# Gated delta rule on one core: where the steps of the neighbouring projections stand among the waits of the chunk inverse

## What is computed

```
proj = h @ w_in                      # q, k (8 heads), v, z (16 heads), b, a
q, k, v = silu(causal_conv(...));  q, k are normalised
a_low = strict((k*beta) @ k.T * decay)        # chunks of 64 tokens
t_inv = inverse(eye + a_low)
u = t_inv @ (v*beta);  w = t_inv @ (k*beta*exp(gc))
per chunk: v_new = u - w @ state
           o = q_dec @ state + attn_intra @ v_new
           state = state*exp(gl) + k_tail.T @ v_new
x = x + (rmsnorm(o) * silu(z)) @ w_o
```

## Time and profile before

| | us |
|---|---|
| median of 3 runs | 1586.14 (1583.64 to 1587.31) |
| the profiled execution, its own time | 1573.19 |
| its span | 1571.4 |
| PE busy | 1516.2 (96% of the span) |
| DVE busy | 560.7 (36%) |
| ACT busy | 378.9 (24%) |
| POOL busy | 189.1 (12%) |
| mean granted TensorE clock | 0.989 of full speed |

### The profile page before, as it was taken

How to read it: one execution, slowest core, us unless ns; L and a number is a source line. 1 busy time by engine, 2 the same in 40 slices (tenths; PEclk the granted TensorE clock), 3 DMA queues, 4 the chain that set the end, 5 groups by cost and what they waited for, 6 DMA issues and landing times.

```text
span 1571.4 us, 34876 instructions
## 1 busy us (share of the span) xinstructions
PE 1516.2 (96%) x15613; PEld 897.7 (57%) x15613; DVE 560.7 (36%) x802; ACT 378.9 (24%) x603; POOL 189.1 (12%) x182
## 2 busy tenths in 40 slices
PE   8799999998999998999999999999999999999997
PEld 6677888776878786753533534444434335345344
DVE  4645444576766757332211212121111112111113
ACT  5544444473645454220000000000000000000000
POOL 0100000114342516000000000000000000000100
PEclk9899999999999999999999999999999999999999
DMA  9218555543142300499999999999999999999993
GB/s 350 92 53 273 188 187 188 163 158 108 55 135 81 132 4 1 156 415 408 411 410 408 411 411 409 410 410 397 411 413 403 412 402 409 412 389 413 414 404 159
DMA packets 145354, 450.38 MB, mean 287 GB/s; under 512 B 10624, under 2 KB 41888, under 8 KB 130880
## 3 DMA queue, kind: packets, MB, share of 16 engines
q1 hardware_dynamic: 141680, 437.10, 72.0%
q0 software_dynamic: 3536, 11.14, 1.8%
HBM read 440.87 MB, written 7.34 MB: 285 GB/s over the span
## 4 chain that ended last, share of the span: by engine, by line
PE 86%; DVE 8%; issue 2%; ACT 1%; SPq 1%; DMA 1%; POOL 1%; POOLq 0%; DVEq 0%; ACTq 0%
PE banks L1929 37%; PE banks L1946 19%; PE banks L1452 8%; PE banks L1454 7%; PE banks L1453 7%; PE banks L1849 1%; PE banks L1839 1%; DVE cvall L1139 1%; DVE wlo L955 1%; PE banks L1830 1%; DMA par<-in_attn_sinks_dram 1%; DVE T L1199 1%; SPq L409 1%; PE banks L1886 1%; PE banks L1858 0%
## 5 line engine op out<-in xcount | busy, mean ns | idle before, releaser
L1929 PE MATMUL banks<-ring,xg 128*32 128x512 f32 (+1 forms) x6144 | 583.2, 539 | 0.0
L1929 PEld LDWEIGHTS banks<-ring,xg 128*32 128x32 f32 x6144 | 199.2, 110 | 367.7 <-issue 331.2
L1274 DVE TENSOR_TENSOR ehid<-banks,esil 64x768 f32<-64x768 f32 (+1 forms) x64 | 89.5, 1399 | 714.9 <-ACT esil L880 714.4
L1946 PE MATMUL banks<-ring,ehT 128*32 128x256 f32 x5376 | 296.1, 379 | 0.0
L1946 PEld LDWEIGHTS banks<-ring,ehT 128*32 128x32 f32 x5376 | 173.8, 110 | 121.3 <-issue 9.7
L880 ACT ACTIVATE esil<-banks 64x1536 f32<-64x1536 f32 (+1 forms) x32 | 41.0, 1282 | 776.7 <-PE banks L1929 776.7
L955 DVE TENSOR_TENSOR wlo<-raw,whi 128x2048 fp32r<-128x2048 f32 x74 | 179.3, 2424 | 80.5 <-ACT whi L635 80.4
L1452 PE MATMUL banks<-whi,xhi 128*128 128x512 f32 x448 | 183.0, 409 | 4.6 <-issue 2.3
L1454 PE MATMUL banks<-whi,xlo 128*128 128x512 f32 x448 | 176.1, 393 | 0.0
L1453 PE MATMUL banks<-wlo,xhi 128*128 128x512 f32 x448 | 175.8, 392 | 0.0
L635 ACT CAST whi<-raw 128x2048 fp32r<-128x2048 f32 x74 | 141.1, 1906 | 47.1 <-PE banks L1454 41.8
(11 more groups left out here) (307 smaller groups left out, 1260.0 us busy)
## 6 DMA issues: line engine op xcount, KB each, us to landing
ring<-in_moe_w_gate_dram SPq DMA_DIRECT2D x112, 1024.0 KB, 15.7
ring<-in_moe_w_up_dram SPq DMA_DIRECT2D x112, 1024.0 KB, 16.3
ring<-in_moe_w_down_dram SPq DMA_DIRECT2D x112, 1024.0 KB, 15.0
raw<-in_dn_w_in_dram SPq DMA_DIRECT2D x16, 1024.0 KB, 5.1
raw<-in_ffn_w_gate_dram SPq DMA_DIRECT2D x22, 512.0 KB, 4.2
raw<-in_ffn_w_up_dram SPq DMA_DIRECT2D x22, 512.0 KB, 5.1
raw<-in_ffn_w_down_dram SPq DMA_DIRECT2D x11, 1024.0 KB, 4.9
raw<-in_dn_w_in_dram SPq DMA_DIRECT2D x16, 512.0 KB, 4.4
```

The costliest lines, as they stand in the source:

```text
L1274: i = dve.tensor_tensor(ehid[64 * s:64 * s + 64, 0:TILES * n_ // 2].rearrange("p (t k j) -> p t k j", t=TILES, k=k_), by_row(src, s), by_r ...
L1929: last = pe.matmul(bank[first_bank + t][TILE * q:TILE * (q + 1), 0:n_].rearrange("p (s c) -> p s c", s=2), xg[:, t, kt, :], w[q // 2][:, k ...
L1946: i = pe.matmul(token_tile(3, t, q, 256), eT[:, h_:h_ + TILE], w[:, at_:at_ + 256], start=first and m == 0 and k == 0 and t % 2 == 0, stop ...
```

## The change

It rewrites the table. There is one more place ahead of the levels, between the products k times q and k and the transposes of the decayed q, and one more late place, behind the new values of block 1. For group 0, 31 steps instead of 26 are done ahead of the levels, and for group 3 all 32 instead of 26, so that its levels hold none. In groups 1 and 2 the count ahead of the levels stays 32, but two steps stand behind the products of line 1802 instead of ahead of them. The tables for line 764 and line 1131 follow.

```
-        FULL_GROUP = ((8, 12, 16, 20, 24, 29, 32), ((34, 36), (38, 40), (42, 44), (46, 48), (50, 53), (56, 58)), (61, 64))
-        FILLED = (((8, 12, 16, 20, 22, 25, 26), ((27, 28), (30, 32), (33, 35), (36, 38), (39, 41), (43, 44)), (46, 48)),
+        FULL_GROUP = ((8, 12, 16, 20, 22, 25, 29, 32), ((34, 36), (38, 40), (42, 44), (46, 48), (50, 53), (56, 58)), (61, 63, 64))
+        FILLED = (((8, 13, 17, 21, 23, 28, 29, 31), ((32, 33), (34, 36), (37, 39), (39, 41), (41, 43), (43, 44)), (46, 47, 48)),
                   FULL_GROUP, FULL_GROUP,
-                  ((6, 10, 16, 20, 24, 25, 26), ((27, 27), (28, 28), (29, 29), (30, 30), (31, 31), (32, 32)), (32, 32)))
+                  ((8, 12, 17, 21, 22, 24, 30, 32), ((32, 32),) * 6, (32, 32, 32)))
         QK_BLOCK0, OUT_BLOCK0 = (1, 2, 3, 5), (4, 6, 7)
-        QK_PART_AT, OUTPUTS_AT = (2, 3), ((0, 0), (4, 5), (4, 5), (3, 6))
+        QK_PART_AT, OUTPUTS_AT = ((1, 2), (2, 3), (2, 3)), ((0, 0), (4, 5), (4, 5), (1, 2))
...
-                        if more and lv == QK_PART_AT[b]:
+                        if more and lv == QK_PART_AT[g][b]:
                             projected_qk(g + 1, b)
...
                 i.then_inc(sem("kk_psum"), 1)
+                filling(5)
                 pe.wait_ge(sem("scaled"), 3 * g + 1)
                 for m in range(8):
                     i = pe.transpose(bank[4 + m // 4][:, m % 4 * P:(m % 4 + 1) * P], qdec[:, m, :], ident)
                 i.then_inc(sem("qdT_psum"), 1)
-                filling(5)
+                filling(6)
...
-                filling(6)
+                filling(7)
...
                         new_values(1)
+                        filling_late(2)
                     pe.wait_ge(sem("v_ready"), g * TB + b + 1)
```

## The result

The changed kernel takes 1588.01 us (median of 20 runs, 1584.41 to 1592.92), the kernel before 1583.64 (20 runs); the ratio is 1.0028, with a 95% interval of 1.0022 to 1.0034. The change makes the kernel 4.4 us slower. The forecast was 1.2 us more, within a range of 1582.5 to 1592.0. The median lies in that range, but the difference is just beyond the 0.2% within which most of the chance had been put.

A forecast was written before the change was run, and what follows sets the result against it. The bound was a chain of waits, in the delta rule on DVE ahead of the levels and on PE in them. Groups gave -1.3 + 1.25 + 1.25 + 0.0 = +1.2 us, so 1587.3, range 1582.5 to 1592.0.

The forecast's parts named there:

- the step on the clock: Group 3's emptied levels, with little waiting, were taken to hold 2.4 GHz; the sum held no clock cost.
- Step 16: Groups 0 and 3: now ahead of line 1782, it waits for ACT's reading of z, costing 3.15 and 3.0 us.
- the step ahead of line 1775 in group 0: Step 12, moved ahead of line 1775's transposes into a PE wait of 1.00 us, was claimed free.
- The rival that was given 0.2: Clock falls in group 3's emptied levels or behind the new waits: slower, about 1591 us; chance 0.2.
- the text's own signs of being wrong: E unmoved relative to convolution, X right behind the cast, group 3 levels at 3.5 or more, or granted clock below 1.0.
- the emptied levels: Group 3's levels without steps; by the skill's rule the dangerous place for the clock, but forecast to hold 2.4 GHz.
- Step 23 and X: Groups 1 and 2: DVE's addition to X waits for step 23, now behind line 1802, 1.9 us later each.
- allowed 0.3 for POOL: Groups 1 and 2: loss could be 0.3 us less if POOL left DVE alone during its wait for step 23.
- Group 3 ahead of the levels: Step 16's wait for z and step 23 holding X together delay the first level by 5.0 us.
- The levels: Each step taken out saves about 0.8 us (0.7 in group 0's level 2): 3.8 in group 0, 5.0 in group 3.
- Level 1: Group 3's first level, 5.27 us before, was to gain 1.0, as DVE's cast stays ahead of its copy of P.
- The late step: Groups 0 to 2: a step fits PE's 0.68 us wait for ACT's vnew, gaining 0.7 us in each group.

The follow-up runs named there:

- e1_z16: Changed kernel with step 16 back behind line 1782 in groups 0 and 3 (16 steps instead of 17 at place 2); 0.9962 of the kernel before's time.
- e5_late: Kernel before with only the late step added, behind the new values of block 1 in groups 0 to 2; 0.9989 of the kernel before's time.
- e6_g3: Kernel before with only group 3's levels emptied, step 16 and step 23 staying where they were; 0.9977 of the kernel before's time.
- e7_x20: Changed kernel with four steps instead of two behind the products of line 1802 in groups 1 and 2; 1.0028 of the kernel before's time.
- e2_x24: Changed kernel with step 23 back ahead of the products of line 1802 in groups 1 to 3; 1.0004 of the kernel before's time.
- e8_cast: Changed kernel with steps 16 and 23 put back, and group 3's last dense-panel cast moved from level 1 to its end; 0.9921 of the kernel before's time.

## Why the forecast was right, and where it was off

- **The mechanisms** in the sum were those that the traces show: gains in the levels of groups 0 and 3 and at the late place, and costs from step 16 and step 23. They nearly cancel, so that the sum is small, as forecast. What failed is the step on the clock, which took 2.4 GHz throughout and gave the clock no term.
- **Step 16** was forecast at +3.15 and +3.0. The start of line 1782 behind the first transposes moved by 18.69 - 15.48 = 3.21 and 19.23 - 15.89 = 3.34. e1_z16 confirms the cause by taking it away, and shows that the step ahead of line 1775 in group 0, which the text called free, and the two in group 3 are gains of 0.67 and 0.81 that only this wait hides.
- **The clock** is the term that was missing from the sum: 1.20 + 1.63 = 2.83 of the 2.9 between forecast and stretch. The text named the wait of 3.0 as new and dangerous but took the rows' side, arguing from the wait of 3.49 in group 0 that had passed without a fall. One such pass was no proof: behind that same wait the clock fell in e5_late and e6_g3, and behind the wait for z in group 0 it fell in the changed kernel and in e7_x20, but not in e2_x24. Of the eleven waits of PE of 2.9 to 3.5 in the stretches of all the profiles, nine were followed by a fall. The rival that was given 0.2 came true in the changed kernel, in its second place, behind the new waits, and so did one of the text's own signs of being wrong, a granted clock below 1.0 in these groups. The place that the text thought the more dangerous, the emptied levels, held 2.4 GHz in seven of the eight profiled kernels that have them and lost it in e1_z16, for 2.44. The prediction cites the Trainium skill (TensorE: Matmul & The Clock Gate, Part 1) for the rule that activity releases the throttle. The traces agree with it behind the waits; in the levels of the changed kernel, where PE was busy for 11.98 of 13 us, it gave no fall.
- **Step 23 and X** in groups 1 and 2: DVE's wait is 1.95, forecast 1.9. The levels came only 1.59 later, for DVE's T took 1.75 instead of 2.67, with POOL's E out of its way, while the cast took 3.23 instead of 2.85; and 0.17 of the 1.59 is what e5_late loses there too, without any change to step 23. The text had allowed 0.3 for POOL. e7_x20 added two more steps to the wait and showed a larger return.
- **Group 3 ahead of the levels**: +6.46 less 1.63 for the clock is 4.83, forecast 5.0. Without the clock, both parts ahead of the levels are within 0.2 of the forecast.
- **The levels** were each forecast at 0.8 per step, and gave 0.71 in levels 2 to 6 of group 3 and 3.51 for five steps in group 0. The term is mis-sized by 0.1 for each level without a step: a step and the change of products took 0.90, but without it PE waits a little. In level 2 of group 3 the second products start 1.17 behind the start of the T products, where the step had started 0.97 behind them, so 0.20 of the 0.90 stays; by ACT's rows (its two Tc copies take 0.81 from 624.08, the products start at 624.59) it is the copy for the first pair of heads. (The bounds also counted ten emptied halves; there are nine, three in group 0 and six in group 3.) Level 1 was forecast at 1.0 and gave 0.85, held by DVE's cast as the text said; e8_cast shows that the cast is worth 1.4.
- **The late step** was forecast at 0.7 and gave 0.67 or 0.68 in each of the three groups.
- **The closeness is partly luck.** Without the clock, the stretch would have moved by 4.10 - 2.83 = 1.27, against 1.2 forecast; but the levels came 0.9 short, and X gave back 0.6. And 1587.3 lies 0.7 below the measured 1588.01 only because it was added to a median of three runs, 1586.14; the kernel before takes 1583.64 over 20 runs, and from there the same sum gives 1584.8, 3.2 short. The range was wide enough to take in the missing term.

## What to carry to other kernels

When work is moved into a wait, look at what the moved piece itself waits for: a step that is free behind a short instruction can cost its whole wait ahead of it, for everything that stands behind it on that engine's queue. A second look belongs to the engine that is released by the step's completion, since it may stand ahead of the critical chain in that engine's own order. The two costs here came from a few counts in the table (17 steps where 16 cost nothing, 22 where 24 did), and the same table without them gains 0.7%. And when the change makes a new wait on PE, a trace in which a like wait passed at the full clock is one case and no rule: give the fall a term or a chance of its own, and look at more than one execution.

## What was not expected of the hardware

- PE idle for 2.92 us between dense products lost the clock in two executions and kept it in a third with the same order around it; a wait of 3.48 or 3.49 lost it in two and kept it in a third. With twelve spare products in the wait for z it was kept in both groups.
- The clock also fell once in levels of small products, 0.50 from 616 to 622 in e1_z16, where seven other kernels held 1.00.
- A POOL product of 128x1024 took 4.47 when it started beside DVE's cast, and 2.36 or 2.37 when it started while DVE was idle; the DVE cast of 128x2048 took from 2.28, with POOL idle, to 3.23. So a wait on one of the two is paid back in part on the other: in e7_x20 0.95 of a further wait of 1.39.
- The profiled execution of the kernel before ran its expert layer 9.7 us faster than the changed kernel's did, for the same instructions, and all the other profiles agree with the latter within 2 us. What makes this difference was not looked into.
